# Context units on three pairs of banks with scores two ahead, a first panel's rest made by GpSimd, six scalings ahead of the last update

## What is computed

```python
def layer(x, cx, ..., need_ctx):
    ...
    px = split_cols(hx @ w_in)
    pc = split_cols(hc @ w_in)
    ya, yca = global_gqa(px[0], px[1], px[2], pc[0], pc[1], pc[2], cos, sin, qn, kn, need_ctx)
    yb, ycb = neighbourhood_attn(px[3], px[4], px[5], pc[3], pc[4], pc[5], rpb, need_ctx)
    yc_, ycc = window_gqa(px[6], px[7], px[8], pc[6], pc[7], pc[8], cos, sin, sink, need_ctx)
    ux = jnp.concatenate([ya, yb, yc_], axis=-1) * jax.nn.silu(px[9])
    x = x + gate[:, None, :] * (ux @ w_out)
    if need_ctx:
        uc = jnp.concatenate([yca, ycb, ycc], axis=-1) * jax.nn.silu(pc[9])
        cx = cx + gate_c * (uc @ w_out)
    return x, cx
```

## Time and profile before

| | |
|---|---|
| median of 3 runs | 2345.12 us (2344.96 to 2345.4) |
| profiled execution, time | 2343.62 us |
| its span, first to last instruction | 2341.8 us |
| TensorE, ScalarE, VectorE, GpSimd busy | 98%, 43%, 60%, 20% |
| mean granted TensorE clock | 0.998 |

### The profile page before, as it was taken

The page is one execution under the profiler, slowest core; times in us unless marked ns, Lnnn a source line. Parts: engine busy times, 40 slices in busy tenths (PEclk is TensorE's granted clock), DMA queues, the critical chain, the costliest instruction groups (busy, mean ns, idle before and its releaser), DMA issues.

```text
span 2341.8 us, 39975 instructions
## 1 busy us (share of the span) xinstructions
PE 2300.3 (98%) x15942; PEld 1902.9 (81%) x15942; DVE 1401.3 (60%) x2818; ACT 1011.9 (43%) x1750; POOL 464.9 (20%) x291
## 2 busy tenths in 40 slices
PE   8999999999999999999999999999999999999998
PEld 7878878788888888888887688888888768888887
DVE  5878776787136766453388558847857755333333
ACT  5773375723247527653455442222235535221221
POOL 2102212022441131214752420000014232000001
PEclk9999999999999999999999999999999999999999
DMA  7303413042222151112241125445442112323222
GB/s 308 143 2 145 171 47 127 2 189 98 67 92 78 59 198 57 55 64 90 86 157 62 56 91 198 167 148 185 170 142 82 55 54 90 100 78 112 99 83 70
DMA packets 64201, 250.51 MB, mean 107 GB/s; under 512 B 7408, under 2 KB 9968, under 8 KB 54544
## 3 DMA queue, kind: packets, MB, share of 16 engines
q1 hardware_dynamic: 61216, 236.10, 29.0%
q0 software_dynamic: 2592, 11.54, 1.5%
q10 hardware_dynamic: 208, 0.33, 0.0%
HBM read 243.67 MB, written 4.19 MB: 106 GB/s over the span
## 4 chain that ended last, share of the span: by engine, by line
PE 89%; ACT 4%; DVE 3%; issue 2%; DVEq 1%; DMA 1%; POOL 1%; ACTq 0%; SPq 0%
PE ps L2948 41%; PE ps L2744 13%; PE ps L2729 8%; PE ps L2925 6%; PE ps L621 4%; PE ps L730 4%; ACT probs L937 3%; PE ps L671 3%; PE ps L715 1%; PE ps L2758 1%; PE ps L2965 1%; PE ps L2615 1%; DMA stage_low<-in_ada 1%; DVEq L820 1%; PE ps L2781 1%
## 5 line engine op out<-in xcount | busy, mean ns | idle before, releaser
L2948 PE MATMUL ps<-h_split,split_panels 128*128 128x512 f32 x2088 | 500.0, 394 | 1.2 <-ACT projected L1788 0.8
L2948 PEld LDWEIGHTS ps<-h_split,split_panels 128*128 128x128 f32 x2088 | 387.9, 188 | 92.8 <-issue 14.7
L1251 POOL TENSOR_TENSOR split_panels_first<-panels_first,split_panels_first 128x1024 fp32r<-128x1024 f32 (+2 forms) x100 | 220.8, 2208 | 728.9 <-ACT split_panels_first L1468 728.9
L2744 PE MATMUL ps<-h_split_first,split_panels_first 128*128 128x256 f32 (+1 forms) x1680 | 294.4, 337 | 0.0
L2744 PEld LDWEIGHTS ps<-h_split_first,split_panels_first 128*128 128x128 f32 x1680 | 258.3, 190 | 34.3 <-issue 1.0
L1269 POOL TENSOR_TENSOR probs_turned<-probs_turned,probs 128x512 f32<-128x512 f32 x30 | 40.0, 1332 | 764.3 <-ACT probs L1731 761.7
L2729 PE MATMUL ps<-h_split_first,split_panels_first 128*128 128x512 f32 (+1 forms) x900 | 190.5, 370 | 0.9 <-POOL h_split_first L1290 0.9
L2729 PEld LDWEIGHTS ps<-h_split_first,split_panels_first 128*128 128x128 f32 x900 | 156.3, 189 | 32.4 <-issue 3.0
L2243 DVE TENSOR_TENSOR split_panels<-panels,split_panels 128x1024 fp32r<-128x1024 f32 (+2 forms) x110 | 127.7, 1164 | 89.0 <-ACT split_panels L1493 88.9
L1920 ACT ACTIVATE probs<-ps 128x512 f32<-128x512 f32 x44 | 26.3, 599 | 349.8 <-PE ps L2948 349.7
L1493 ACT ACTIVATE split_panels<-panels 128x1024 fp32r<-128x1024 f32 (+2 forms) x149 | 144.7, 979 | 67.0 <-PE ps L2948 63.0
(11 more groups left out here) (341 smaller groups left out, 3964.7 us busy)
## 6 DMA issues: line engine op xcount, KB each, us to landing
panels<-in_w SPq DMA_DIRECT2D x88, 512.0 KB, 3.7
modulation_panels<-in_ada SPq DMA_DIRECT2D x40, 1024.0 KB, 4.9
panels_first<-in_in SPq DMA_DIRECT2D x72, 512.0 KB, 4.8
late_modulation_panel<-in_ada SPq DMA_DIRECT2D x24, 1024.0 KB, 4.8
panels<-in_in SPq DMA_DIRECT2D x42, 512.0 KB, 3.7
panels_first<-in_out SPq DMA_DIRECT2D x32, 384.0 KB, 3.1
panels<-in_w SPq DMA_DIRECT2D x32, 384.0 KB, 3.5
panels<-in_w SPq DMA_DIRECT2D x32, 320.0 KB, 2.9
```

The source lines that it names most:

```text
L1251: nc.gpsimd.tensor_tensor(flat1(n, 1)[:, s], raw1[:, n % RAW1, s], flat1(n, 0)[:, s].bitcast(F32), ALU.subtract).then_inc(rest1_done, 1)
L2744: ins = mm(to, split1[:, s, w, c, :], hs1[:, h, c, lo:lo + n], start=c == 0 and i == 0, stop=c == KC - 1 and i == 2)
L2948: ins = mm(out, panel_of(n, l)[:, a, c - base, :], moving(b, c), start=first and i == 0 and j == 0, stop=last and i == len(chunks) - 1 and ...
```

## The change

1. In A and C the context units (`small`) take pairs of banks, (6, 7), (2, 3), (4, 5) in turn. Their scores are issued a step earlier: in the first context unit's step the next unit's scores stand at the end, from then on the following unit's scores stand at the beginning of each step. They wait for the last users of both banks. On ScalarE the copy of prev follows u's exponentials where both are context units.
2. At the seam the rest of the first panel of layer 1 is made by GpSimd in two pieces of 512 columns, ahead of its chunks of h; VectorE's L2114 goes. TensorE waits for the front piece ahead of its third matmul, and for the other at chunk 4. The second panel follows two chunks behind, not three.
3. In the tail the first half's scalings 2 to 5 stand ahead of the second half's update, and its reciprocal behind scaling 7.

```diff
+        u["small"] = bool(small_sets) and len(u["tiles"]) == 2
+        u["users"] = []
+        if u["small"]:
+            u["set"] = small_sets[n_small % len(small_sets)]
+            n_small += 1
+            u["users"] = [user[b] for b in u["set"]]
+        for b in u["set"]:
+            user[b] = (u, b == u["set"][-1] and len(u["set"]) == 3)
...
+                                          small_sets=None if m == "B" else ((6, 7), (2, 3), (4, 5))), at["u"])
...
-            if u["banks_of"] and u["in_sets"]:
+            if u["small"]:
+
+                for other, third in u["users"]:
+                    ev = other["events"][-1 if third else 0]
+                    pe.wait_ge(pt_by_act if ev["by"] == "act" else pt_by_dve, ev["c"] + 1)
+            elif u["banks_of"] and u["in_sets"]:
...
-                if u and not (m == "C" and i == 1):
+                following = {x["unit"]["i"]: x["unit"] for x in steps if x["unit"]}.get(i + 1) if u and u["small"] else None
+                if u and u["small"] and prev["small"]:
+                    if following:
+                        scores_pe(pe, following, o)
+                elif u and not (m == "C" and i == 1):
                     scores_pe(pe, u, o)
...
+                if following and not prev["small"]:
+                    scores_pe(pe, following, o)
...
-                copies_last = u and len(u["set"]) == 2
+                copies_last = u and prev and len(u["set"]) == 2 and len(prev["set"]) == 2
...
+                    first_panel = main_no[IN1, l, 0]
+                    pool.wait_ge(rounded1, first_panel + 1)
+                    for lo, e, made in ((0, FRONT, front_rest), (FRONT, 2 * FRONT, rest1_done)):
+                        nc.gpsimd.tensor_tensor(flat1(first_panel, 1)[:, lo:e], raw1[:, first_panel % RAW1, lo:e],
+                                                flat1(first_panel, 0)[:, lo:e].bitcast(F32), ALU.subtract).then_inc(made, 1)
...
-                        if (j, c) == (0, 1):
-                            main_rest(main_no[IN1, l, 0])
...
-                    if (h, c) == (0, 1):
+                    if (h, c) == (0, 5):
                         update_half(r, 1, 4, mod2[:, DEPTH - 1, 40 + KC - 1:40 + KC], out_ready, out1_done + DEPTH * OUTS2)
-                    if (h, c) == (0, 5):
+                    if (h, c) == (0, 7):
                         over_half_roots(r, 1)
...
-                    late = 5 if j else 3
+                    late = 5 if j else 2
...
+                                if (j, b, c, i) == (0, 0, 0, 2):
+
+                                    pe.wait_ge(front_rest, front_rest_no[n_panel])
```

More of the change, by code:

```diff
@@ L94, with make_plan @@
 BANKS_TURNED = 3
-def make_plan(groups, at, banks, sets=None, score_banks=None, out_bank=1, late=False, values_second=None):
+def make_plan(groups, at, banks, sets=None, score_banks=None, out_bank=1, late=False, values_second=None, small_sets=None):
     steps, ring, copies = [], [], []
@@ L174, in make_plan @@
     last_of = [units[-1] for _, units in groups]
+    n_small, user = 0, {}
     for i, (g, u) in enumerate(flat):
@@ L546, in two_dit_blocks @@
                 sets = ((6, 7), (4, 5), (2, 3)) if m == "B" else ((5, 6, 7), (2, 3, 4))
-                plans[l, m] = (make_plan(groups, at, (0,) if m == "B" else (0, 1), sets, values_second={"A": "behind", "C": "behind"}.get(m)), at["u"])
+                plans[l, m] = (make_plan(groups, at, (0,) if m == "B" else (0, 1), sets, values_second={"A": "behind", "C": "behind"}.get(m),
+                                          small_sets=None if m == "B" else ((6, 7), (2, 3), (4, 5))), at["u"])
         start2 = dict(at)
@@ L612, in scores_pe @@
             last = {}
-            third = u["banks_of"]["events"][1:] if u["banks_of"] and u["in_sets"] else []
+            third = u["banks_of"]["events"][1:] if u["banks_of"] and u["in_sets"] and not u["small"] else []
             for e, col, a, z in segments(u):
@@ L1063, in two_dit_blocks @@
         front_no = {n: i + 1 for i, n in enumerate(in_halves)}
+        front_rest_no = {n: i + 1 for i, n in enumerate(sorted([*in_halves, *(main_no[IN1, l, 0] for l in range(1, DEPTH))]))}
         def columns(n):
@@ L2775, in blocks_by_parts @@
                             if (j, b, c) == (0, 1, 0):
-                                pe.wait_ge(front_rest, front_no[n_panel])
-                            if (j, b, c) in ((0, 0, 0), (0, 1, KC // 2)):
+                                pe.wait_ge(front_rest, front_rest_no[n_panel])
+                            if (j, c) == (0, KC // 2):
                                 pe.wait_ge(rest1_done, n_panel + 1)
                             for i, (w, h) in enumerate(((0, 0), (0, 1), (1, 0))):
+                                if (j, b, c, i) == (0, 0, 0, 2):
+                                    pe.wait_ge(front_rest, front_rest_no[n_panel])
                                 ins = mm(bank(2 * j + k % 2, 0, n), split1[:, main_no[IN1, l, b] % SPLIT1, w, c, :], hs1[:, h, c, lo:lo + n],
@@ L2805, in project @@
                     if b == 2:
-                        pe.wait_ge(front_rest, front_no[main_no[IN1, l, b]])
+                        pe.wait_ge(front_rest, front_rest_no[main_no[IN1, l, b]])
                     else:
```

## The result

| | before | after |
|---|---|---|
| median | 2344.68 us (2342.9 to 2346.25, 20 runs) | 2348.76 us (2347.78 to 2352.35, 20 runs) |
| profiled execution, span | 2341.8 us | 2347.3 us |

The ratio is 1.0019, 95% interval 1.0013 to 1.0026: the change makes the kernel 0.19% slower, just inside the bound of 0.2%. The forecast was 2348.7.

What follows compares the result with a forecast made beforehand. TensorE, busy 98% of the span, was taken as the bound, so only its waits count. +5.0 - 0.5 - 0.9 = +3.6 us on 2343.62 gives 2347.2, plus 1.5 to the median: 2348.7, range 2344.0 to 2351.0.

Steps and rivals of the forecast that it cites:

- First part, +5.0: Context units of A and C: scores wait for a later copy, A +2.7 us and C +2.3 us, bounds +3.5 to +5.8.
- the loop: Context units: transposes, two exponentials, copy, waiting scores, next transposes; 2.75 us in A against 2.27, 2.57 in C against 2.10.
- The 0.47: Context units: time in us from transposes to ScalarE when the transposes are not stalled, taken for A and C.
- The rivals' condition: Context units: the copy does not reach the scores late, being taken ahead by ScalarE or the banks being free.
- rival 2: Context units: VectorE sets the pace, 2.12 us a unit in A, some 1.9 in C; total 2342.3 us; 10%.
- Rival 3: Context units: as fast as TensorE can, 1.8 us a unit in A and C; total 2338.7 us; 4%.
- Second part, -0.5: Seam between the layers: VectorE's subtraction goes, GpSimd makes the rest, second panel joins one step earlier; gain 0.5 us.
- the blocking of the two engines: Seam: GpSimd and two-SBUF-input VectorE operations block each other, a GpSimd piece taking 1.83 us instead of 1.28.
- its bounds 1.4 and -0.9: Seam: gain of 1.4 us without blocking, loss of 0.9 us with blocking at every pair of operations.
- Third part, -0.9: Tail: fewer scalings before the second half's reciprocal and earlier output transfers; gain 0.9 us, between 0.3 and 1.2.
- 0.4 in the final scaling: Tail: nothing stands between the reciprocal and the second half, so the final scaling ends 0.4 us earlier.
- 0.5 in the landing: Tail: first 512 KB goes out some 2.2 us earlier, so the last output piece no longer queues; 0.5 us taken.

Runs made afterwards that it cites:

- the last two kernels: Against the kernel before: context units reordered (exponentials, scores, VectorE's minimum earlier) plus tail part, 2340.51 us; the same plus seam part and a tiny VectorE copy, 2341.57 us.

## Why the prediction came out right

**First part, +5.0: right in mechanism, measured +5.5.** A's transposes started at 164.59, 170.58 and 179.18 us where the prediction had 164.81, 170.9 and 179.1, and the last at 183.25 (183.4): +2.70 against +2.7. C came to +2.84 against +2.3. The term that was mis-sized is the loop, 2.87 and 2.69 against 2.75 and 2.57: from the transposes to ScalarE 0.54 instead of 0.47, the copy with its way to TensorE 0.72 instead of 0.64, the scores 0.51 instead of 0.54. The 0.47 was one row at the entry of the stage. Five loops in C make 0.6 of it; in A an earlier start made up for it. The rivals' condition, that the copy is ahead or the banks free, was tried apart: the copy ahead gives before's pace, and the scores behind the transposes give VectorE's, rival 2. Rival 3 named the pace of TensorE, 1.8; with VectorE's minimum moved ahead as well, the units went to 1.92 and 1.84, with TensorE never idle.

**Second part, -0.5: +0.3 in the profiled execution; the step that failed is the clock, priced at full speed throughout.** Chunk 1 was taken up at 680.89 on before's clock (681.0 forecast). The rows bear out the blocking of the two engines: GpSimd's two pieces take 2.99, not twice 1.28, and VectorE's half of h 1.07 at 682.82, not 0.75. One by one, GpSimd's first piece takes 1.30, to 683.34; VectorE's half, started within it, ends 0.55 behind that, at 683.89; and GpSimd's second, started at 683.30, takes 1.73. The Trainium skill, SBUF — State Buffer, section SBUF: two separate sides, has this as an exclusive lock: whichever of the two starts first keeps the shared port pair for its whole instruction. The trace agrees, 1.30, then 1.07, then 1.73. With the clock held the part gained 0.83, against the 0.5 of the forecast and within its bounds 1.4 and -0.9; with 3.4 us at half clock it lost 0.32 to 0.37 in each of four executions. Besides, the part takes one instruction out of VectorE's row, and that cost 0.7 far away, which nothing in the prediction had.

**Third part, -0.9: -1.0**, and -1.0 alone. It was put together from 0.4 in the final scaling and 0.5 in the landing. The last scaling ends 8.78 us behind the first half's spread, where it was 9.06, so it gave 0.3; the landing gave the other 0.7, as its 2.2 against 2.9 us show. (2.10 MB at 348 GB/s are 6.0 us and not 6.1; nothing hangs on it.)

**The sum.** +5.0 - 0.5 - 0.9 = +3.6 was forecast; the profiled spans say +5.4, the medians of 20 runs +4.1. That 2348.7 met 2348.76 is luck. The sum was put on a median of three runs, 2345.12, which lay 0.44 above that of 20; and it was 0.48 short of the +4.08 between the medians. Of the terms, the seam's 0.8 and the 0.7 of VectorE's stalls were missing, and the loop was 0.5 short; against them the profiled execution of before lay 1.1 below its median and that of after 0.3 above. "No change can be told" held for the bound of 0.2%; the interval of the 20 runs, 1.0013 to 1.0026, does tell the slowdown from none.

**Open.** Whether the seam's pause makes the clock fall. Of thirteen profiled executions of all these kernels, five have the seam part with its pause of 1.35 and no added matmuls, and in four of them the clock fell 0.8 to 2.0 us behind the pause's end, for 3.4 us each time; in the seven without the seam part it never fell there. TensorE's idle time as such is not it: those seven stand still more at the seam, 1.20, 0.17, 0.49 and 0.90 us one behind the other, against 0.65 and 1.35. And with the pause filled the clock fell ahead of the seam; it fell in four of the thirteen at 1177 to 1186 us, the seam part in or not. The kernel before is not free of it either: of its 21 runs beside the last two kernels, nine have a mean clock of 0.996 and a median of 2345.48 us, nine have 0.997 and 2343.82, three have 0.998 and 2343.77. What makes the stalls of 0.43 us is open too; shown is only where they stand in VectorE's row. And whether the gain of the context units needs the third pair of banks was not tried: every run with a new order has three.

## What to carry to other kernels

Here more buffers and an earlier issue helped only together with the order on the engine that frees the buffers: before moving work ahead in an in-order queue, follow what it waits for around the whole loop, because a wait moved in front of something that was ready costs its full length on each pass. When one wait is removed, look up the next pace by engine: here, once the scores stood behind the transposes again, it was VectorE's minimum, and once that was moved too, TensorE's own row. The two moves together turned a loss of 5.5 us in the two stages into a gain of 2.1. And where an edit takes even one instruction out of an engine's row, compare offsets along the whole trace, not only at the edit and not only the two spans.

## What the runs showed of the hardware

VectorE stands still for 0.41 to 0.45 us at ten or twelve places of its row, the same from run to run, releaser "issue". In these kernels all but one are at every 128th record plus 63, waits and drains counted, and that one is a record later. Other instructions fall on these places when one is taken out ahead of them, and the old ones when a small one is put in its place. Two such shifts cost 0.33 and 0.35 us each time; the other seven places where one went or came (five went, two came) show no step above 0.05 us, so those are hidden.

Granted TensorE clock: stretches of 3.4 us at the lower level occur in single executions at two seams (680 to 692 and 1177 to 1186 us), once with no pause ahead of them. One costs about 1.1 us at the seam between the layers (7.08 to 7.12 against 5.94 us for the same matmuls) and 0.7 to 0.8 at the later one.
